# Gathering tokens for four experts at a time, in four PSUM banks, and starting the last experts' gate and up products early

## What is computed

```python
s = jax.nn.sigmoid((t @ w_router).astype(F32))
sel = s + router_bias
...
gates = jnp.sum(jax.nn.one_hot(idx, N_EXPERTS) * w[..., None], axis=1)
def expert(y, p):
    wg, wu, wd, ge = p                     # 1024x512, 1024x512, 512x1024
    a = jax.nn.silu(t @ wg) * (t @ wu) * ge[:, None]
    return y + a @ wd, None
y, _ = lax.scan(expert, jnp.zeros_like(t), (w_gate, w_up, w_down, gates.T))
```

## Time and profile before

| | us |
|---|---|
| median of 3 runs | 1482.36 (1480.48 to 1483.65) |
| the profiled execution, its own time | 1484.81 |
| its span, first to last instruction | 1483.0 |
| PE busy in it | 1379.9 (93%) |
| L940, gathers, 768 instructions, both layers | 106.4 |
| L1043 with L1044 beside it, 384 each, on the ring | 170.1 |
| L1074 with L1075 beside it, 192 each, on the ring | 92.4 |
| DVE, ACT busy | 425.8, 278.9 |

### The profile page before, as it was taken

One profiled execution on the slowest core, in us unless ns is written; L12 is line 12 of the kernel. 1 busy time (PEld: TensorE's weight loads), 2 busy tenths in 40 slices (PEclk: granted clock), 3 DMA queues, 4 the chain that ended last, 5 costly groups with the idle time before them and its releaser, 6 DMA issues.

```text
span 1483.0 us, 17019 instructions
## 1 busy us (share of the span) xinstructions
PE 1379.9 (93%) x6528; PEld 715.8 (48%) x6528; DVE 425.8 (29%) x1242; ACT 278.9 (19%) x576; POOL 46.5 (3%) x63
## 2 busy tenths in 40 slices
PE   5999999998999998899999999998699898889997
PEld 2455566655444443544544544544465544344434
DVE  3045265433111113420611603503211411111124
ACT  3043254311100110410211202202111110001113
POOL 1001200000000001000100100000000000000010
PEclk9999999998999999999999999999799899999999
DMA  9977686847999999822332322333032799569891
GB/s 355 309 273 235 202 299 243 332 139 261 399 397 355 397 378 399 301 107 71 107 114 100 128 69 102 114 114 131 11 114 104 259 398 396 202 237 398 304 400 50
DMA packets 162737, 344.76 MB, mean 232 GB/s; under 512 B 5929, under 2 KB 23554, under 8 KB 162626
## 3 DMA queue, kind: packets, MB, share of 16 engines
q1 hardware_dynamic: 150320, 319.19, 58.7%
q10 hardware_dynamic: 9362, 14.37, 2.6%
q0 software_dynamic: 2944, 9.65, 2.4%
HBM read 324.96 MB, written 18.22 MB: 231 GB/s over the span
## 4 chain that ended last, share of the span: by engine, by line
PE 86%; DMA 4%; DVE 4%; ACT 2%; SPq 2%; issue 1%; DVEq 0%; ACTq 0%
PE psum L762 19%; PE psum L1043 14%; PE psum L755 11%; PE psum L1074 7%; PE psum L940 7%; PE psum L1173 6%; PE psum L891 3%; PE psum L1158 3%; PE psum L657 2%; PE psum L985 2%; DMA ring<-in_da_w_qkv 2%; SPq L559 1%; DMA ring<-in_moe_w_up 1%; PE psum L1014 1%; DMA ring<-in_w_ada 1%
## 5 line engine op out<-in xcount | busy, mean ns | idle before, releaser
L762 PE MATMUL psum<-ring,hT 128*128 128x512 f32 x672 | 289.4, 592 | 0.0
L762 PEld LDWEIGHTS psum<-ring,hT 128*128 128x128 f32 x672 | 127.7, 190 | 159.0 <-issue 157.8
L755 PE MATMUL psum<-hT,ring 128*128 128x384 f32 x512 | 172.7, 496 | 9.4 <-DMA ring<-in_da_w_qkv 6.5
L1043 PE MATMUL psum<-ring,work 128*64 128x512 f32 x384 | 170.1, 593 | 1.4 <-DMA ring<-in_moe_w_up 1.4
L1044 PE MATMUL psum<-ring,work 128*64 128x512 f32 x384 | 170.1, 593 | 0.0
L755 PEld LDWEIGHTS psum<-hT,ring 128*128 128x128 f32 x512 | 98.5, 194 | 77.7 <-issue 7.6
L940 PE MATMUL psum<-work 128*128 128x128 f32 x768 | 106.4, 291 | 6.9 <-issue 4.9
L940 PEld LDWEIGHTS psum<-work 128*128 128x128 f32 x768 | 94.8, 199 | 29.8 <-issue 25.7
L1043 PEld LDWEIGHTS psum<-ring,work 128*64 128x64 f32 x384 | 51.9, 137 | 109.7 <-issue 109.5
L1074 PE MATMUL psum<-ring,work 128*64 128x512 f32 x192 | 92.4, 626 | 1.8 <-issue 1.7
L1075 PE MATMUL psum<-ring,work 128*64 128x512 f32 x192 | 92.6, 627 | 0.0
(11 more groups left out here) (325 smaller groups left out, 1599.0 us busy)
## 6 DMA issues: line engine op xcount, KB each, us to landing
ring<-in_w_ada SPq DMA_DIRECT2D x24, 2048.0 KB, 12.3
ring<-in_moe_w_gate SPq DMA_DIRECT2D x24, 2048.0 KB, 12.6
ring<-in_moe_w_up SPq DMA_DIRECT2D x24, 2048.0 KB, 15.6
ring<-in_moe_w_down SPq DMA_DIRECT2D x24, 2048.0 KB, 16.6
ring<-in_da_w_qkv SPq DMA_DIRECT2D x6, 2048.0 KB, 17.2
sq<-in_moe_w_gate SPq DMA_DIRECT2D x8, 1536.0 KB, 12.3
hT<-in_moe_w_up SPq DMA_DIRECT2D x8, 1536.0 KB, 14.7
work<-in_moe_w_down SPq DMA_DIRECT2D x24, 512.0 KB, 11.5
```

Source lines behind the costliest of these rows:

```text
L755: last = mm(b[:, 0:TOK], w[:, kt, col:col + P], hT[:, kt, :], start=kt == 0, stop=kt == KT - 1)
L762: last = mm(b, hT[:, kt, P * t:P * t + P], w[:, kt, :], start=kt == 0, stop=kt == KT - 1)
L1043: mm(psum[0:BLK, x, :], xk, wg[kt], start=kt == 0, stop=kt == KT - 1)
```

## The change

The gather is done for four experts at once: `sel` has 4 x 64 = 256 columns, each gather matmul moves 256, and a group of four experts takes 24 matmuls. Part x of it (2 of the 8 tiles of width) goes to bank 2, 3, 4 or 7. `xs` has one buffer for four experts. In experts 0 to 11 PE does one part per expert for the next group, 4 matmuls ahead of the transposes and 2 behind. Part 3 uses the overflow bank 7, so PE waits for DVE's `free7` before it, in experts 3, 7 and 11. ACT copies all four parts in experts 3, 7 and 11: two between silu and the copy of the transposed block, two behind that. Experts 12, 13 and 14 have nothing to gather and do 2 + 1 of the 8 tiles of the next expert's gate and up product there instead. `side_work` of expert 15 moves from tiles 1, 3, 5, 7 to 4, 5, 6, 7. Two small buffers share their place with others (`pick` with `w`, `hi` with `selb`), which changes no instruction.

```diff
-    plan = {(e, 2 * i + 1): pair(e - 1, i) for e in range(LAST + 1, NE) for i in range(4)}
+    plan = {(e, AHEAD + 1 + i): pair(e - 1, i) for e in range(LAST + 1, NE) for i in range(4)}   # AHEAD = 3, QUAD = 4
...
+        GBANK = (2, 3, 4, 7)
...
-                def gather(half, kts):
-                    for kt in kts:
-                        out = psum[:, 2 + half, P * (kt % 4):P * (kt % 4) + P]
-                        for t in range(TT):
+                def gather(x, first, end):
+                    for i in range(first, end):
+                        kt, t = 2 * x + i // TT, i % TT
+                        out = psum[:, GBANK[x], 256 * (kt % 2):256 * (kt % 2) + 256]
...
+                def gate_up(e, kts):
+                    wg, wu = unit(e, 0), unit(e, 1)
+                    for kt in kts:
+                        if e % QUAD == 0 and kt % 2 == 0:
+                            pe.wait_ge(m["xs"], e + kt // 2 + 1)
+                        xk = xs[:, kt, BLK * (e % QUAD):BLK * (e % QUAD) + BLK]
+                        mm(psum[0:BLK, e % 2, :], xk, wg[kt], start=kt == 0, stop=kt == KT - 1)
+                        last = mm(psum[BLK:P, e % 2, :], xk, wu[kt], start=kt == 0, stop=kt == KT - 1)
...
+                    gate_up(e, range(AHEAD if e > NE - QUAD else 0, KT // 2))
+                    hint = pe.mark_branch_hint_location()
+                    wg, wu = gate_up(e, range(KT // 2, KT))
+                    overflow(e, wg, wu, hint)
+                    if more:
+                        pe.wait_ge(m["sel"], quad + 2)
+                        pe.wait_ge(m["xs"], e + 1)
+                        if e % QUAD == QUAD - 1:
+                            pe.wait_ge(m["free7"], quad + 1)
+                        gather(e % QUAD, 0, 4)
+                    elif e + 1 < NE:
+                        gate_up(e + 1, range(AHEAD - 1))
+                    pe.wait_ge(m["gated"], e + 1)
...
+                    if more:
+                        gather(e % QUAD, 4, 6).then_inc(m["gathered"], 1)
+                    elif e + 1 < NE:
+                        gate_up(e + 1, range(AHEAD - 1, AHEAD))
+                    wd = unit(e, 2)
...
+                            if next_quad:                      # ACT, between silu and the transposed copy
+                                take_xs(it + 1, 0)
+                                take_xs(it + 1, 1)
...
+                            if next_quad:                      # ACT, behind it
+                                take_xs(it + 1, 2)
+                                take_xs(it + 1, 3)
...
                             V.tensor_tensor(ea[0:BLK, x, :], sg[BLK:P, x, :], psum[BLK:P, x, :], ALU.mult).then_inc(m["gated"], 1)
                             overflow(e, lo, hint)
+                            if e % QUAD == QUAD - 1 and e + 1 < NE:
+                                dve.sem_inc(m["free7"], 1)
```

More of the change, by code:

```diff
@@ L1403, in overflow @@
                                                   oy[OVB * j:OVB * j + OVB, :]).then_inc(m["o_stored"], 16)
-                take_xs(0, 0, 0)
-                take_xs(0, 0, 1)
+                for x in range(QUAD):
+                    take_xs(0, x)
                 act.wait_ge(m["routed"], 1)
@@ L1891, in experts @@
                         q = it * 2 + par
-                        if q + 1 < NE // 2:
-                            dve.wait_ge(m["gathered"], q * 2 + 2)
-                            select(q + 1)
+                        if par == 0 and it + 1 < NQUAD:
+                            dve.wait_ge(m["gathered"], QUAD * it + QUAD)
+                            select(it + 1)
                         for x in range(2):
```

113 lines of the change are left out of this document (48 added, 65 removed).

## The result

The changed kernel takes **1519.65 us** (median of 4 runs, 1518.06 to 1520.83) where the kernel before takes 1481.42 beside it: a ratio of 1.0242, 95% interval 1.0219 to 1.0265. It is slower by 36 us by that ratio and by 38 between the two medians; 20 had been predicted.

What follows compares the result with a forecast made beforehand. PE was taken to bound the chain almost everywhere, with weight loads (DMA share 1.00) a second limit in the first expert stage. Layer delays of +10.9 and +9.4 us, together +20.3, on 1482.4 gave 1503 us, range 1490 to 1512.

Steps and rivals of the forecast that it cites:

- long waits: PE waits for up weights ahead of the transposes of experts 13 and 14, both layers: some 7 and 6 us.
- First gathers: Before expert 0 of each layer: gathers 12.1 us instead of 7.5, select +0.5, together +5.1 us per layer.
- Gathers beside an expert: Experts 0 to 11: 12 gathers of 256 columns replace 3.07 us, -0.48 us each, -5.8 us for twelve.
- Bank-7 wait: Experts 3, 7 and 11: PE waits for VectorE's mark before the gather, 1.5 us each, 1.2 at layer 1's expert 7.
- Issue 12: SP's weight issue behind expert 12's transposes: +3.3 us in layer 0, +3.0 in layer 1.
- From issue 12 to silu of 15: Last four experts: filler waits close the load loop; silu of 15 starts 10.9 us later in layer 0, 9.4 in layer 1.
- crowding of the combinations: Expert 15: combinations stand closer together, one per pair column; at most 0.5 us, left out of the sum.
- the clock would not fall (1): Long waits at experts 13 and 14 leave the PE clock up: +12.3 us, 1495; chance 0.12.
- weights would follow faster (2): Last experts' second unit of a pair arrives after 14.3 us instead of 15.6 and 16.3: +14.3 us, 1497; chance 0.08.
- Rival 3: Short waits at experts 3, 7 and 11 also halve the clock, 1.7 us each, six times: +30 us, 1513; chance 0.06.
- faster outcome (5): Both units of the last experts arrive 8.6 us after issue, so no filler waits: -15.5 us, 1467; chance 0.05.
- rival 4: No change: stream never restarts, clock holds, bank-7 mark comes at once; layer 0 +6.2, layer 1 -5.1, 1483.5 us; chance 0.07.

Runs made afterwards that it cites:

- e8: Changed kernel with 7 dummy matmuls of 512 columns ahead of the filler of experts 13 and 14, keeping PE busy in the long waits: 1513.47 us, ratio 1.0194.
- e6: Changed kernel with every 256-column gather split into two of 128 columns: 1525.63 us, ratio 1.0282.
- s2: Kernel before with 43 small matmuls (172 instructions) ahead of PE's first instruction, where PE is idle: 1498.67 us, ratio 1.0098.
- e4: Changed kernel with SP releasing gate and up slots on VectorE's mark behind the product instead of PE's transposes: 1504.31 us, ratio 1.0132.
- e7: Changed kernel with all three filler tiles behind the transposes and ahead of the down product: 1510.83 us, ratio 1.0188.
- s1: Kernel before with 22 small matmuls (88 instructions) ahead of PE's first instruction, where PE is idle: 1487.32 us, ratio 1.0021.
- e10: Kernel before with dummy matmuls on PE while it waits for the routing and in two steps of the retention tail: 1492.08 us, ratio 1.0066.
- s4: Changed kernel with 43 small matmuls ahead of PE's first instruction, where PE is idle: 1522.86 us, ratio 1.0260.

## Why the prediction was wrong in size

The direction and the main mechanism were right: a loop that had slack was closed, and the four long waits are where they had been placed and as long as they had been placed. Step by step:

**First gathers: right.** 12.61 us were measured for 12.1, and the select's part was 0.4 for 0.5; 12.25 us in layer 1.

**Gathers beside an expert: the step that failed.** The prediction took 18 + 6 gathers at 3.07 us and set against them 12 x 0.215 = 2.58, a gain of 0.48 us per expert. The measured rows are 1.99 + 1.13 = 3.12, and the rows of before that answer to them 2.27 + 0.94 = 3.21. The price of one instruction was right (0.216 start to start, 0.112 for 128 columns), but it is the price inside a row of them. The 3.07 was taken from the start of a row to the start of what follows it and holds some 0.2 us more for each row, at its head and its end (24 x 0.112 is 2.68); the 2.58 holds none of that. Set start to start, silu of expert 0 to silu of expert 1, with the change:

```profile
361.39 0.59 ACT L1430 ACTIVATE work<-psum 64x512 f32<-64x512 f32 x1 [5.13 <-PE psum L1045]
375.22 0.59 ACT L1430 ACTIVATE work<-psum 64x512 f32<-64x512 f32 x1 [11.14 <-PE psum L1045]
```

And in the kernel before:

```profile
354.81 0.59 ACT L1415 ACTIVATE work<-psum 64x512 f32<-64x512 f32 x1 [5.13 <-PE psum L1044]
368.75 0.59 ACT L1415 ACTIVATE work<-psum 64x512 f32<-64x512 f32 x1 [9.86 <-PE psum L1044]
```

13.83 us for 13.94; the other undisturbed experts of both layers have 13.82 or 13.83 for 13.91. So the gain was 0.08 us per expert, 1.0 per layer instead of 5.8: **4.8 us per layer, 9.6 of the 14.4 that are missing between the profiled executions.** e6 says the same from the other side: with 128 columns again the step is 13.91. The Trainium skill ("TensorE: Matmul & The Clock Gate", section "Back-to-back issue gap") gives columns / 2.4 + 2.5 ns for an isolated matmul at full clock, and more, 81 ns, for 128 columns in a stream with its weight loads. As an estimate from the first of these, with each of the two instructions of a float32 matmul counted as two such gaps, 128 columns take 0.112 us and 256 take 0.218, and the wider gather saves 0.07 us per expert. The rows agree with this (0.112 and 0.216) and not with the 81 ns, of which two would be 0.162.

**Bank-7 wait: right in kind, short by 1.** 1.5 was taken, 1.67, 1.98 and 1.98 are measured in layer 0: 5.6 us for 4.5. The third is followed by a stretch at 1.2 GHz of 3.4 us, which cost 1.6 more (silu of 11 to silu of 12 takes 17.45 us, 3.62 over 13.83). In layer 1 it is 4.8 for 4.2, with 1.16 at the overflowed expert 7 for the 1.2 predicted.

**Issue 12: wrong in layer 0, right by two errors in layer 1.** From the first gather it comes 9.4 us later in layer 0, where 2.8 were predicted. In layer 1 it is 2.7 for 2.5, but that is luck: the gathers again gained 4.8 us too little, and the 1.94 us wait of the kernel before and its slow clock, 5.4 us together, did not recur. The prediction had named this as open in its spread.

**The long waits: right.** 6.99, 6.82, 7.25 and 6.69 for 7 and about 6. The up load took 15.02 us from its issue for 15.3. Behind the first wait four pairs and the transposes took 4.2 us (573.32 to 577.54), where 2.1 is their time at 2.4 GHz: a clock loss of 2.1, and 0.2 in the next pair, for the 2.0 taken. e8 puts all four at about 7 us, where the prediction took 8.

**From issue 12 to silu of 15: short by 2.3 and 1.5.** 53.1 and 52.8 us for 50.8 and 51.3. About 0.5 is the crowding of the combinations that had been left out:

```profile
604.54 0.92 PE L1018 MATMUL psum<-work 64*128 64x384 f32 x4
...
606.40 1.45 PE L1018 MATMUL psum<-work 64*128 64x384 f32 x4
```

**Not in the sum but for the wider select: the rest of the span,** +4.9 us, of which the two selects are 0.8. Ahead of the first select the work is the same in all kernels but those with added matmuls, and still the first gather starts between 338.4 and 345.1 us in the profiled executions. The span without the two stages is 937.2 to 941.7 us in the runs built on the kernel before and 938.6 to 947.0 in those built on the changed one. So a difference of this size comes from unrelated edits too; how much of it is the change's no run tells.

**The terms together,** in us: 9.6 for the gathers, 3.3 for bank 7 with its slow clock, 3.8 behind issue 12, 0.7 for the first gathers and 4.1 outside the stages are 21.5 too little. Waits and slow clock that only the kernel before has, 5.4 in layer 1 and 1.7 in layer 0, take 7.1 off again, which leaves the 14.4. Without them the prediction would have been further off.

**The rivals.** That the clock would not fall (1) and that weights would follow faster (2) are refuted by the rows above. Rival 3, slow clock behind the short waits, is true for one of six. The faster outcome (5) needed a load within 8.6 us of its issue; it takes 15.5. In rival 4 the +4.5 of layer 1 does not follow from the terms given (9.4 less two clock losses of 2.0 is 5.4), which changes nothing here. What none of them held is that 172 instructions added where PE is idle move this kernel by 15 us (s2). Over three layouts each, by medians, the kernel before has 1483.7, 1487.3 and 1498.7, the changed one 1519.7, 1520.9 and 1522.9, and the gather alone 1502.2, 1499.8 and 1495.7. The layout in which the kernel before stands is the best of its three. Between the means of the three the change costs 31 us.

**Still open.** Why the changed kernel meets fewer waits for code: it has 384 gather instructions where there were 768, but e6, with 768 again, caught one wait and not many. Also what decides how early PE asks for a block; that the waits stand mostly just behind the overflow branch is seen, not explained.

## What to carry over

Work that is pulled forward as filler brings its waits with it. If it stands ahead of the step that releases the next load, load and release form a loop, and each turn of it costs the whole latency of the load; move the release ahead of it (e4) or the filler behind it (e7) first, then ask whether the filler still pays. Price a change of instruction width by start-to-start times of a whole period, since a row's duration has a fixed part that does not scale. And before a difference under 1% between two builds is given to a cause, shift the program by some instructions and look whether the difference is still there.

## What the runs showed of the hardware

- The page counts an instruction queue on the same 16 DMA engines as the weights, with packets of 16 KB. By s1 and s2 PE can stand still for the next one: 1.3 to 3.7 us in most cases, 3.5 with no other transfer under way, 3.3 (s2) and 6.7 (e10) with the queues full. The profile gives such a wait to nothing ("issue"); its sign is a packet of the instruction queue that ends 1.2 to 1.7 us before PE goes on.
- Adding 172 instructions at a place where PE is idle made the kernel 15 us slower, 1.0% (s2). In layer 0, where 14 of them arose, such waits and the stretches at 1.2 GHz behind them account for it.
- Two gathers of 128 columns and one of 256 cost PE nearly the same: 24 in 3.21 us and 12 in 3.12.
- A wait of 1.98 us was followed by a stretch at 1.2 GHz at expert 11 and not at expert 7 of the same layer; in s4, with the same waits, it was the other way round. Waits of 6.3 us and more for weights were followed by one each time in these kernels.
